# One step of a hybrid decoder trunk on eight cores: weight loads issued singly and tied to TensorE's progress around the token-major projections

## What is computed

```
for i in range(4):
    f = swiglu(rmsnorm(h, g[0]), ffn_w_in[i, 0], ffn_w_down[i, 0]);  h = h + 0.5 * rmsnorm(f, g[1])
    m = mixer_i(rmsnorm(h, g[2]));                                   h = h + rmsnorm(m, g[3])
    f = swiglu(rmsnorm(h, g[4]), ffn_w_in[i, 1], ffn_w_down[i, 1]);  h = h + 0.5 * rmsnorm(f, g[5])

def swiglu(x, w_in, w_down):
    gate, up = split(x @ w_in);  return (silu(gate) * up) @ w_down
```

## Time and profile before

| | us |
|---|---|
| median of three runs | 5160.59 |
| the three runs | 5142.51, 5160.59, 5391.1 |
| the profiled execution's own time | 5130.61 |
| its span, slowest core (core 0) | 5129.0 |
| spans of the eight cores | 5046.2 to 5129.0 |
| TensorE busy on core 0 | 4679.5 (91%) |
| VectorE, ScalarE, GpSimd busy | 1763.9, 1210.7, 623.7 |

### The profile page before, as it was taken

One profiled execution on the slowest core, in us unless ns is written; L12 is line 12 of the kernel. 1 busy time (PEld: TensorE's weight loads), 2 busy tenths in 40 slices (PEclk: granted clock), 3 DMA queues, 4 the chain that ended last, 5 costly groups with the idle time before them and its releaser, 6 DMA issues.

```text
span 5129.0 us, 82003 instructions; the slowest of 8 cores (5046.2 to 5129.0 us)
## 1 busy us (share of the span) xinstructions
PE 4679.5 (91%) x29990; PEld 2746.7 (54%) x29990; DVE 1763.9 (34%) x3001; ACT 1210.7 (24%) x2371; POOL 623.7 (12%) x1098
## 2 busy tenths in 40 slices
PE   7995799998999989998998976999999998999799
PEld 4544455554646445554645553656555554646464
DVE  2244323255232452325222344232542235232422
ACT  2123212122121331214211222121221224121321
POOL 1100101011010120102011101010110112010210
PEclk8897899999999999999998988999999999999999
DMA  8445735355353453533636356453553627443361
GB/s 168 66 67 111 116 62 96 64 94 92 68 94 66 91 97 62 99 66 58 105 95 117 58 109 104 77 93 68 91 105 58 109 54 116 81 85 80 57 107 46
DMA packets 316822, 442.96 MB, mean 86 GB/s; under 512 B 186815, under 2 KB 225855, under 8 KB 316414
## 3 DMA queue, kind: packets, MB, share of 16 engines
q0 software_dynamic: 88592, 319.79, 36.1%
q1 hardware_dynamic: 227838, 117.93, 10.9%
HBM read 682.92 MB, written 12.71 MB: 136 GB/s over the span
## 4 chain that ended last, share of the span: by engine, by line
PE 76%; DMA 9%; DVE 5%; issue 3%; SPq 3%; ACT 2%; POOL 1%; DVEq 0%; ACTq 0%; POOLq 0%
PE ps L177 76%; DMA big<-big 7%; DVE big L177 5%; SPq L133 3%; ACT big L177 2%; DMA big<-wst 1%; DMA big<-xp 1%; POOL big L177 1%; DMA big<-saT 0%; SPq L131 0%; POOL big L133 0%; DVEq L76 0%; ACTq L76 0%; POOLq L76 0%; SPq L76 0%
## 5 line engine op out<-in xcount | busy, mean ns | idle before, releaser
L177 PE MATMUL ps<-big 128*128 128x384 bf16 (+8 forms) x29990 | 4679.5, 328 | 440.0 <-DMA big<-big 204.1
L177 PEld LDWEIGHTS ps<-big 128*128 128x128 bf16 (+2 forms) x29990 | 2746.7, 101 | 2372.2 <-issue 570.3
L177 ACT ACTIVATE big<-ps 128x384 f32<-128x384 f32 (+6 forms) x1467 | 820.4, 561 | 3003.1 <-PE ps L177 2981.4
L177 DVE TENSOR_TENSOR big<-ps,big 128x384 bf16<-128x384 f32 (+3 forms) x1161 | 605.7, 522 | 2047.4 <-PE ps L177 2029.1
L177 DVE SCALAR_TENSOR_TENSOR big<-big 128x1024 f32<-128x1024 f32 (+7 forms) x546 | 573.1, 1053 | 206.1 <-POOL big L177 93.5
L133 POOL DMA_DIRECT2D big<-wst x608 | 329.0, 543 | 2575.3 <-PE ps L177 2500.3
L177 POOL TENSOR_TENSOR big<-big 128x1 f32<-128x1 f32 (+2 forms) x434 | 282.5, 652 | 1838.4 <-DVE big L177 1836.9
L177 ACT ACTIVATE big<-big 128x1024 bf16<-128x1024 f32 (+5 forms) x385 | 321.6, 855 | 758.8 <-DVE big L177 661.9
L177 DVE TENSOR_SCALAR big<-big 128x1 f32<-128x1 f32 (+3 forms) x456 | 81.3, 179 | 762.9 <-ACT big L177 739.4
L177 DVE SCALAR_TENSOR_TENSOR big<-ps,big 128x1024 f32<-128x1024 f32 (+7 forms) x277 | 295.3, 1066 | 137.8 <-POOL big L177 114.6
L177 DVE TENSOR_TENSOR big<-big 128x384 bf16<-128x384 f32 (+13 forms) x120 | 80.5, 676 | 49.3 <-ACT big L177 18.1
(11 more groups left out here) (7 smaller groups left out, 8.0 us busy)
## 6 DMA issues: line engine op xcount, KB each, us to landing
big<-wst POOLq DMA_DIRECT2D x608, 512.0 KB, 7.9
big<-gains SPq DMA_DIRECT2D x52, 512.0 KB, 8.3
big<-big SPq DMA_DIRECT2D x192, 71.0 KB, 2.1
big<-xp SPq DMA_DIRECT2D x16, 512.0 KB, 8.6
yp<-big SPq DMA_DIRECT2D x16, 512.0 KB, 2.7
big<-big SPq DMA_DIRECT2D x64, 70.8 KB, 2.2
big<-big SPq DMA_DIRECT2D x48, 64.0 KB, 2.0
big<-big SPq DMA_TRANSPOSE x158, 2.8
```

The lines of the kernel that those rows point to most:

```text
L177: return lambda e: getattr(e, name)(*args, **kwargs)
```

## The change

A load no longer starts whenever a slot is free. The pump is also run, as `S.hook`, at each `S.pump`. A `cast` entry is issued only if 7.5 modelled us have passed since the last one (`PACE`), or if the modelled clock is past `WS.slow`; `tok_mm` and both `outp` set `WS.slow` to 40 us behind the modelled end of their projection. A forced pump at the start of the program, and `w_get` and `lent_open` for an entry that is not issued yet, issue without that condition. Every `cast` load names, as a read, the newest operation that was emitted for TensorE, so GpSimd's queue waits until TensorE has done that one.

```diff
+PACE = 7.5
+SLOW = 40.0
     def pump(self):
+        self.hook()
         while self.heap and self.heap[0][0] <= self.now:
...
-        def w_pump():
-            while WS.nxt < min(len(plan), WS.limit) and WS.free:
...
+        def w_issue():
+            k = WS.nxt
+            key, kind, arg = plan[k]
+            s = WS.free.pop(0)
+            WS.slot[k] = s
+            if kind == 'cast':
+                rd = []
+                if p.ecount['pe'] > 0:
+                    p.lastw['petick'] = (('e', 'pe'), p.ecount['pe'])
+                    rd = ['petick']
+                p.dma('pool', [(A.at(slot_off(k), [SLOT_EL], BF16), wst[arg])], ('w', s), reads=rd, writes=[('ws', s)])
+                WS.due = S.now + PACE
+            elif kind == 'raw':
+                p.dma('sp', [raw_src(arg, k)], ('wr', s), writes=[('ws', s)])
+            WS.nxt += 1
+
+        def w_pump(force=False):
+            while WS.nxt < min(len(plan), WS.limit) and WS.free and (force or plan[WS.nxt][1] != 'cast' or S.now >= WS.due or S.now > WS.slow):
+                w_issue()
+
+        S.hook = w_pump
 
         def w_get(key, shape, dt=BF16):
             k = PIDX[key]
+            while WS.nxt <= k:
+                w_issue()
...
         def tok_mm(g_, taus, lhs, lhs_ids, keys, nk, spawn):
             MODE.chain = 'B'
+            WS.slow = S.now + SLOW + sum(4 * MM(512) * len(keys) for t in taus)
...  (mixer A, ahead of its last projections)
+            WS.slow = S.now + SLOW + 20.0
             outp(taus[4:6], False)
...  (mixer C, ahead of its projections)
+            WS.slow = S.now + SLOW + 35.0
             outp(nts[0].taus, False)
...  (start of the program, and the two later steps of it)
                 WS.limit = 2
-                w_pump()
+                w_pump(True)
```

More of the change, by code:

```diff
@@ L528, in build_program @@
             limit = 0
+            due = 0.0
+            slow = 0.0
             free = list(range(RING))
```

## The result

The changed kernel takes 4976.7 us (median of four executions, 4971.8 to 5000.5) beside 5142.5 us (median of three) for the kernel before on the same chip. The ratio is 0.968, with a 95% interval of 0.963 to 0.973. Run again on two other chips it gave 0.970 [0.968, 0.973] and 0.971 [0.968, 0.975].

The account below looks back on a forecast made before the run. TensorE was taken as the bound, idle 440.0 us, much of it awaiting transposes. Terms 47 + 70 + 22.5 + 5 + 25 + 13.5 - 6 = 177 us gave a 4952 us span; forecast 4962 us, range 4895 to 5055.

Parts of the forecast that it names:

- 1 down projections: Ends of feed-forward down projections leading into another feed-forward: all six stalls waiting for transposes go, 47 us.
- 2 mixers: Ends of the mixers: 70 of 79 us of stalls go, 3 us staying in each second-group mixer.
- 3 between the groups: Between the two groups, the last tile's new x lands sooner: 22.5 of 25.0 us of waiting go.
- 4 saT: Before mixer A of the first group, TensorE's wait for the state saT: 5 of 9.4 us go.
- 5 clock: Lower granted clock in the 12 us after each of 15 stalls: 25 of 30 us come back.
- 6 layer 3: Layer 3's late feed-forward weights: 13 us of waiting instead of 26.6, so 13.5 us won.
- 7 GpSimd's queue, mixer C: Loads held back by the tie at the start, in `d_prep` and mixer C: four places, 6 us lost.
- 8 burst after 40 us: About eight loads issued together 40 us after a projection meet the feed-forward's steady stretch: zero cost.
- rival A: One load is enough to hold a transpose, some 15 us; mixers keep over half their stalls: about 5010 us, chance 0.15.
- B: Weight ring runs dry, five late loads at each of 14 projections cost 392 us: 5354 us, chance 0.05.
- C: Nothing moves: loads bunch behind TensorE's ticks and transposes crawl as before, about 5140 us, chance 0.06.
- D: Denser work lowers the clock to 0.81 and eats the gain: 5140 us, or 5315 if doubled, chance 0.04.

Follow-up runs that it names:

- the last experiments: Changed kernel with 3.5 spacing for first loads after layer 3's and 2's first down projections, some first loads held 9 us: 4946.2 with mixer A copy spacing, 4926.8 without.
- the fours: Changed kernel with loads issued four at a time every 30 modelled us instead of singly every 7.5: lowest 5001.0 us.
- the tie alone: Changed kernel with spacing set to 0, every load still waiting for TensorE's newest operation: 5114.3 us, ratio 1.001 of the kernel before.

## Why the prediction was right

The forecast was 4962 us and the measured time 4976.7. Core 0, on which the sum was made, allows a check of each step; waits under 2 us are not counted.

| step | forecast, us | measured on core 0, us |
|---|---|---|
| 1 down projections | 47 | 47.0, all six stalls gone |
| 2 mixers | 70 | 79.0 - 2.3 = 76.7 |
| 3 between the groups | 22.5 | 25.0 - 3.2 = 21.9 |
| 4 saT | 5 | 9.38 - 6.05 = 3.3 |
| 5 clock | 25 | 24.5 |
| 6 layer 3 | 13.5 | 26.6 - 2.46 - 5.80 - 5.72 = 12.6 |
| 7 GpSimd's queue, mixer C | -6 | -3.31 - 2.65 = -6.0 |
| 8 burst after 40 us | 0 | 0 |
| sum | 177 | 180.0, less 2.7 of other waits: 177.3 |
| stretches at a clock of 0.81 | not in the sum | 10.5 |
| span of core 0 | 177 | 187.8 |

- **Steps 1 to 3** rest on one bound: a transpose beside one load lands after at most 8.6 us. On core 0, 3 of 158 took longer than 8 us, the longest 9.58 (before: 37 of 158, the longest 37.17). The bound held there for one load (7.3 us at most); the two above it had three and four in flight. Over all eight cores the longest beside one load took 13.6 us. The 7.9 us of the transpose in the profile after is about the 2.8 us of a transpose alone plus the 5.0 us of a load alone: the two share the engines, and neither is held for longer than the work of both. That is also why step 2 came out better than 70: the 3 us charged for each mixer of the second group fell due in one of three.
- **Why many loads hold a transpose** was right in its kind and wrong in its size. The prediction lets one packet of the transpose through for each packet of a load. From 828 to 850 us on core 0 of the kernel before, within the 29.47 us of the earlier trace rows, the loads' queue q0 and SyncE's queue q1, which carried that transpose, moved just as many (packets, MB, share of 16 engines):

```profile
q0 software_dynamic: 972, 3.56, 95.2%
q1 hardware_dynamic: 972, 0.25, 9.3%
```

  The 19 us were too few for two reasons. The window of the earlier trace rows ends inside the fourth transpose, so 918 packets are less than one: from 780 to 790 us a whole one moves.

```profile
q1 hardware_dynamic: 1056, 0.26, 33.5%
```

  That is 66 turns for each engine, 66 x 0.33 = 22 us. And its first packet comes late. Over the eight cores of the kernel before, 79 transposes were issued with seven or more loads in flight and no other transpose beside them. In the median their first packet moved 3.9 us after the issue (1.2 us for a transpose alone; why it is later here stays open), from the first to the last took 22.5 us, in which 1054 packets of loads started (1034 to 1120 in all 79), and the landing came 27.6 us after the issue. The transposes of these cores, by how many loads were in flight when they were issued (one load, and the 11 transposes with five, six or ten, are left out):

| loads in flight at issue | transposes | median us to landing | landed after the last of these loads, median us |
|---|---|---|---|
| 0 | 939 | 2.8 | |
| 2 | 30 | 5.9 | 1.6 |
| 3 | 66 | 11.6 | 1.1 |
| 4 | 16 | 11.4 | 0.9 |
| 7 | 12 | 20.2 | 0.6 |
| 8 | 50 | 27.0 | 2.8 |
| 9 | 58 | 27.7 | 1.8 |

  Seven loads have about as many packets as a transpose (7 x 146 = 1022). With fewer ahead, and none behind, they run out first, and the transpose lands right after them; with more it lands when its own turns are done. Loads that are issued behind it hold it too: 63 transposes with one load ahead and three or more issued while they ran took 19.1 us in the median. The eleven that took over 31.5 us, up to 39, all shared SyncE's queue with another transpose; so did the 16.62 us of the earlier trace rows, which rival A puts down to four loads alone. The Trainium skill ("DMA: Bandwidth & Descriptors", Queues, rings and completion order) has an engine go round its queues a packet at a time, where a packet holds several descriptors. The equal counts agree with the taking of turns; how many of the profile's packets make one turn they don't show. For the sum the wrong size made no difference, because a load that is alone holds a transpose for its own few packets only.
- **Step 5** came out at its size, behind a number that hides it. Busy time fell by 35.0 us, but the matmuls of both kernels are the same in the same order, and set side by side on core 0 they say where: 23.3 us come from matmuls that ran at 0.81 in the stretch of the earlier trace rows from 50 to 210 us, 12.9 were lost again in stretches at 0.81 around mixer A of the kernel after, and 24.5 remain. Of these, 29.7 are in the fifteen 12 us stretches of step 5, and 5.2 were lost elsewhere. So the 10.5 us of the level of 0.81 are not the change's work as far as is known, since it comes and goes from execution to execution (below); without them the sum is met almost to the microsecond, which is partly luck, as step 2 gave 6.7 us more than forecast and everything else together 6.4 less. The granted clock is 0.970 on core 0, beside a forecast near 0.965.
- **Step 6** held place by place: a short wait at the first block, then one of 5.8 us for a load that `w_get` forces and that waits for TensorE's newest operation. It was also the clearest thing to mend, as the last experiments show.
- **Step 7** was right in its sum by luck of its parts: mixer C took 6.0 us alone, where I had put 3 on it and 3 on the start and `d_prep`, which cost next to nothing on this core.
- **The waits** for DMAs from SBUF to SBUF came to 67.2 us, not 80 to 90: I had not taken off the 6 and 4.9 us of the earlier trace rows and charged mixers that didn't stall. What I said of mixer A's copies, that no load delays them, was wrong: four loads issued at 2940.1 to 2943.9 us on core 4 meet them, and the first copies take 16 us. SyncE's timeline there, and TensorE's:

```profile
2943.31 27.20 SPq L135 DMA_DIRECT2D big<-big  x24
...
2969.91 30.52 SPq L135 DMA_DIRECT2D big<-big  x43
```

```profile
2965.99 1.26 PE L179 MATMUL ps<-big 128*32 128x256 bf16 x20 [19.29 <-DMA big<-big]
```

  SyncE issues 24 copies in 27.20 us among the loads, 1.13 us each, and then 43 in 30.52 us, 0.71 each. At 0.71 us the first 24 would need 17 us anyway, which may be why spacing these loads did not shorten the wait.
- **From the core to the kernel.** Part of the agreement is not the sum's merit. Core 0 was the slowest before and is not after: the slowest span fell by 155.3 us, not 187.8, for core 4 waits 26.8 us more than core 0 (313.9 against 287.1), 14.1 of them for DMAs from SBUF to SBUF. Averaged over all cores the fall is 137 us. On the other side the before's profiled run lay 12 us below its median of 5142.5, and the after's 1 us; the 8 us that I added for that were about right. So the medians fell by 165.8 us where the forecast had about 177.
- **Rivals.** A fell: over the eight cores of the kernel after, 144 transposes were issued with one load in flight and took 5.1 us in the median, not 15. B showed only in the fours. C is the tie alone, and did not occur with spacing. D: the clock did fall to 0.81 in other places, below, and took 12.9 us on core 0, less than the 23.3 that the same level had taken before.

## What to carry to other kernels

When a stage ends on a small transfer that it waits for, count its packets and the packets of the large transfers queued beside it: here they took turns one for one, so a transpose of 1056 packets landed right behind fewer than seven loads of 146, and after some 27 us beside more. Keep the number of large transfers at one or two at these moments, by spacing the large ones or by taking the small one off the DMA queues; either gave the whole gain here, and a tie to progress or a strictly single issue added almost nothing. Space no wider than that takes, since the time beyond that comes back as late weights: 3.75 modelled us beat 7.5, and four loads every 30 us lost some 43 us of the gain.

## What the hardware showed beyond that

The stretches at a granted clock of 0.81 move about. In the kernel after, core 0 has 0.97 in the stretch of the earlier trace rows that had 0.80, and 0.70 around mixer A, part of it at 0.81 (busy time by stretch; third number from the end is the granted clock):

```profile
50.00:210.00 160.00, 153.67 (x993) 97.23 (x991) 44.86 (x171) 33.04 (x67) 28.41 (x79) 0.97 0.75 129
312.00:515.00 203.00, 137.61 (x1856) 89.99 (x1856) 90.27 (x176) 54.76 (x125) 12.12 (x21) 0.70 0.46 97
```

In the profiled executions of the changed kernel on the other two chips no core has any. The Trainium skill ("TensorE: Matmul & The Clock Gate", Seeing it yourself) has the limiter behind this level hold while dense work lasts on a die's cores; here all eight cores are dense for most of 4900 us and the level comes in a stretch or not at all. What sets it off stays open.
